# Mixture-of-experts loop of a decoder step: another place for the light experts, column groups in the second product, one merged product for the last two experts

## The reference

```
scores = sigmoid(x @ w_router);  idx = top 8 of the allowed groups;  gates = w_sel / sum(w_sel) * 2.5
for each expert e, with the tokens that chose it:
    hb = silu(xb @ w1_e[e]) * (xb @ w3_e[e])          # 1024 -> 256
    out[tokens] += (hb @ w2_e[e]) * gate              # 256 -> 1024
y = swiglu(x, w1_s, w3_s, w2_s) + out
x = layer_norm(ALPHA * x + y)
```

## Time and profile before

| | us |
|---|---|
| median of 3 runs | 1189.84 |
| lowest and highest | 1188.80, 1190.72 |
| the profiled execution | 1188.33 |
| its span | 1186.6 |
| expert loop, first c step to last y step, about | 535 to 1134 |
| loading back, sums and layer norm, about | 1127 to 1187 |

### The profile page before, as it was taken

How to read it: one execution, slowest core, us unless ns; L and a number is a source line. 1 busy time by engine, 2 the same in 40 slices (tenths; PEclk the granted TensorE clock), 3 DMA queues, 4 the chain that set the end, 5 groups by cost and what they waited for, 6 DMA issues and landing times.

```text
span 1186.6 us, 21423 instructions
## 1 busy us (share of the span) xinstructions
PE 1129.1 (95%) x8348; PEld 752.3 (63%) x8348; DVE 427.9 (36%) x1127; ACT 256.9 (22%) x533; POOL 254.0 (21%) x292
## 2 busy tenths in 40 slices
PE   7999996999999988989999999999999999999996
PEld 6888654877875767857765555555555565555521
DVE  0359998233039434661112222122222222221034
ACT  1101144013042124201122222222222222222210
POOL 3120050000000000032333333433323333333300
PEclk9999998999998999999999999999999999999999
DMA  9630304015045652185999999999999999999696
GB/s 331 250 142 1 152 21 177 1 75 227 1 143 176 250 214 108 73 286 197 365 408 392 396 383 394 402 399 388 383 386 402 393 384 384 381 401 387 260 369 279
DMA packets 67593, 319.16 MB, mean 269 GB/s; under 512 B 11591, under 2 KB 17951, under 8 KB 40909
## 3 DMA queue, kind: packets, MB, share of 16 engines
q1 hardware_dynamic: 51269, 278.60, 60.3%
q0 software_dynamic: 14848, 35.48, 7.9%
q10 hardware_dynamic: 1424, 4.35, 0.9%
HBM read 300.15 MB, written 29.36 MB: 278 GB/s over the span
## 4 chain that ended last, share of the span: by engine, by line
PE 74%; DVE 16%; DMA 4%; ACT 2%; SPq 2%; issue 1%; POOL 0%; DVEq 0%; POOLq 0%
PE psum L797 66%; PE psum L812 8%; DVE act_mem L1782 7%; DVE mk_mem L1944 2%; DMA arena<-y_rows 2%; DMA arena<-in_w_in_dram 1%; SPq L572 1%; DMA act_mem<-x_rows,more_x 1%; DVE act_mem L2000 0%; ACT act_mem L1565 0%; DVE act_mem L2151 0%; DVE act_mem L1879 0%; ACT act_mem L1574 0%; DVE act_mem L1796 0%; DVE act_mem L2163 0%
## 5 line engine op out<-in xcount | busy, mean ns | idle before, releaser
L797 PE MATMUL psum<-arena,act_mem 128*32 128x128 f32 (+6 forms) x4800 | 507.8, 361 | 0.9 <-ACT act_mem L1665 0.9
L797 PEld LDWEIGHTS psum<-arena,act_mem 128*32 128x32 f32 (+5 forms) x4800 | 259.7, 123 | 188.8 <-issue 107.9
L797 PE MATMUL psum<-act_mem,arena 128*128 128x260 f32 (+1 forms) x1728 | 355.1, 367 | 8.2 <-DMA arena<-in_w_in_dram 2.8
L797 PEld LDWEIGHTS psum<-act_mem,arena 128*128 128x128 f32 x1728 | 307.9, 194 | 52.8 <-DMA arena<-in_w_in_dram 3.0
L705 POOL DMA_INDIRECT y_rows<-act_mem,idx_y x39 | 45.9, 1177 | 239.3 <-DVE act_mem L2201 226.3
L812 PE MATMUL psum<-ident,act_mem 128*128 128x128 f32 (+6 forms) x484 | 80.0, 297 | 17.2 <-DVE act_mem L1883 6.8
L2201 DVE TENSOR_SCALAR act_mem<-psum,act_mem 96x512 f32<-96x512 f32 (+1 forms) x40 | 29.9, 747 | 159.7 <-PE psum L797 159.7
L1782 DVE SCALAR_TENSOR_TENSOR act_mem<-act_mem,wcb 128x511 f32<-128x511 f32 (+29 forms) x120 | 77.8, 729 | 0.0
L812 PEld LDWEIGHTS psum<-ident,act_mem 128*128 128x128 f32 (+6 forms) x484 | 58.5, 172 | 29.6 <-issue 13.7
L2198 DVE TENSOR_TENSOR act_mem<-act_mem,psum 128x192 f32<-128x192 f32 x35 | 12.4, 355 | 161.2 <-ACT act_mem L1636 161.2
L797 PEld LDWEIGHTS psum<-act_mem 128*96 128x96 bf16 (+7 forms) x419 | 31.3, 125 | 60.7 <-issue 59.7
(11 more groups left out here) (282 smaller groups left out, 789.6 us busy)
## 6 DMA issues: line engine op xcount, KB each, us to landing
arena<-in_w_e_dram SPq DMA_DIRECT2D x192, 1024.0 KB, 9.8
arena<-y_rows SPq DMA_DIRECT2D x8, 2048.0 KB, 24.2
arena<-in_w_in_dram SPq DMA_DIRECT2D x16, 512.0 KB, 18.0
arena<-in_cache_mem_k_dram SPq DMA_DIRECT2D x8, 1024.0 KB, 8.6
arena<-in_cache_mem_v_dram SPq DMA_DIRECT2D x8, 1024.0 KB, 12.1
arena<-in_w_v_dram SPq DMA_DIRECT2D x1, 4096.0 KB, 24.7
arena<-in_w_k_dram SPq DMA_DIRECT2D x1, 4096.0 KB, 14.0
arena<-in_w_out_dram SPq DMA_DIRECT2D x1, 4096.0 KB, 14.0
```

The costliest lines, as they stand in the source:

```text
L797: return pe.matmul(out, lhsT, rhs, start=first, stop=last)
```

## The change

The light places are now third, seventh and eighth of eight (`LIGHT = (2, 6, 7)`), so both of the last two experts are light, and the sixth place is heavy.

The down product of a heavy expert that isn't big is `down_most`: for 64 tokens two column groups of 64 side by side (4 products of 512 columns), for the other 32 tokens four column groups of 32 (8 products of 256 columns). Its result lies in pieces in PSUM, so `yh_most` copies it with three instructions on ACT and three on DVE, in place of one each. As tokens don't lie alone on partitions of that result in a way that one gate could be applied, the gate is now multiplied in DVE's `hd_most`, by two instructions with a per-partition factor in place of one; the factors are laid out by `spread_gates`, six small copies in `i_step`, before `idx_x` is written.

The last two experts' results go to `late_y`, expert 62 on partitions 0 to 63 and 63 on 64 to 127, and are added with 2 products of 128 rows a tile in place of 4. One of the three zero scatters goes.

```
-LIGHT = (2, 5, 7)
-HEAVY = (0, 1, 3, 4, 6)
+LIGHT = (2, 6, 7)
+HEAVY = (0, 1, 3, 4, 5)
...
+            def down_most(b, part):
+                _, wd = ew(part)
+                for k in range(2):
+                    for h in range(2):
+                        mm(psum[LCAP * h:LCAP * h + LCAP, 0, 0:512], hidT[:, b, MCAP * k:MCAP * k + LCAP],
+                           wd[:, k, 512 * h:512 * h + 512], k == 0, k == 1)
+                for k in range(2):
+                    for q in range(4):
+                        last = mm(psum[MORE * q:MORE * q + MORE, 0, 512:768], hidT[:, b, MCAP * k + LCAP:MCAP * k + MCAP],
+                                  wd[:, k, 256 * q:256 * q + 256], k == 0, k == 1)
+                return last
...
                 for h in range(2):
-                    mm(ps[0:w, 512 * h:512 * h + 512], slot_tok[0:MCAP, 0, t * P:t * P + w],
-                       ys[0:MCAP, 0, 512 * h:512 * h + 512], False, False)
-                for h in range(2):
-                    mm(ps[0:w, 512 * h:512 * h + 512], slot_tok[LCAP * h:LCAP * h + LCAP, 1, t * P:t * P + w],
-                       ys[LCAP * h:LCAP * h + LCAP, 1, 0:512], False, False)
+                    mm(ps[0:w, 512 * h:512 * h + 512], slot_tok[:, t * P:t * P + w],
+                       late_y[:, 512 * h:512 * h + 512], False, False)
...
+            def yh_most(out):                                     # DVE; ACT has the same for the other half
+                dve.tensor_copy(out[0:LCAP, 512:1024], psum[LCAP:2 * LCAP, 0, 0:512])
+                for q in range(2, 4):
+                    last = dve.tensor_copy(out[LCAP:MCAP, 256 * q:256 * q + 256], psum[MORE * q:MORE * q + MORE, 0, 512:768])
...
+            def spread_gates(n):
+                for h in range(2):
+                    dve.tensor_copy(gates[LCAP * h:LCAP * h + LCAP, n, 0:1], picked[0:LCAP, n, 1:2])
+                for q in range(4):
+                    dve.tensor_copy(gates[MORE * q:MORE * q + MORE, n, 1:2], picked[LCAP:MCAP, n, 1:2])
...
+            def hd_most(b, n):                                    # it was one tensor_tensor of 192 columns
+                dve.scalar_tensor_tensor(silu[:, b, 0:P], silu[:, b, 0:P], gates[:, n, 0:1],
+                                         psum[:, 2, 512 * b + 192:512 * b + 320], ALU.mult, ALU.mult)
+                return dve.scalar_tensor_tensor(silu[:, b, P:192], silu[:, b, P:192], gates[:, n, 1:2],
+                                                psum[:, 2, 512 * b + 320:512 * b + 384], ALU.mult, ALU.mult)
```

More of the change, by code:

```diff
@@ L243, in decoder_step @@
         swT = act_mem[:, A4 + 1296:A4 + 1296 + T]
+        gates = act_mem[:, A4 + 1860:A4 + 1860 + 2 * NB].rearrange("p (n c) -> p n c", c=2)
         idx_y = sb("idx_y", [P, NB], U32)
@@ L758, in _ @@
                     g_step(e + 3, (e + 3) % NB)
[L759 to L763, removed]
+                if SCATTERED <= e + 3 < E:
+                    scatter_halves((e + 3) % NB, zeros, s_zeroed)
             gp.wait_ge(s_over, 1)
@@ L1310, in y_step @@
                 else:
-                    down(n % 2, n % 4, CAP if is_big(e) else MCAP).then_inc(m_y, 1)
+                    (down if is_big(e) else down_most)(n % 2, n % 4).then_inc(m_y, 1)
             wait_out(pe, "x24")
@@ L1650, in yh, with yh_late @@
                 return act.activation(out[0:cap, 0:512], psum[0:cap, 0, 0:512], ACT.Copy, scale=picked[0:cap, n, 1:2])
+            def yh_late(b):
+                for h in range(2):
+                    last = act.activation(late_y[LCAP * b:LCAP * b + LCAP, 512 * h:512 * h + 512],
+                                          psum[LCAP * h:LCAP * h + LCAP, 0, 0:512], ACT.Copy)
+                return last
+            def yh_most(out):
+                act.activation(out[0:LCAP, 0:512], psum[0:LCAP, 0, 0:512], ACT.Copy)
+                for q in range(2):
+                    last = act.activation(out[LCAP:MCAP, 256 * q:256 * q + 256],
+                                          psum[MORE * q:MORE * q + MORE, 0, 512:768], ACT.Copy)
+                return last
             def sl_few(b):
@@ L1682, in y_step @@
                     act.wait_ge(m_sm[n % 2], 16 * halves_out(i, k - 2, 2))
-                if is_light(n):
+                if isinstance(e, int) and e >= SCATTERED:
+                    yh_late(e - SCATTERED).then_inc(m_ya, 1)
+                elif is_light(n):
                     yh_few(n % 2, n).then_inc(m_ya, 1)
+                elif is_big(e):
+                    yh(ys[:, n % 2, :], n).then_inc(m_ya, 1)
                 else:
-                    yh(ys[:, n % 2, :], n, CAP if is_big(e) else MCAP).then_inc(m_ya, 1)
+                    yh_most(ys[:, n % 2, :]).then_inc(m_ya, 1)
             def step(e, k, i, sc):
@@ L1709, in _ @@
             y_step(E - 1, NB - 1, LAST, 16 * ((E - 1) // 2))
-            for b, cap in enumerate((MCAP, P)):
+            for b in range(2):
                 wait_full(act, f"slots{b}")
-                act.activation(slot_tok[0:cap, b, :], bank(f"slots{b}")[0:cap, 0:T], ACT.Copy).then_inc(s_emA, 1)
+                act.activation(slot_tok[LCAP * b:LCAP * b + LCAP, :], bank(f"slots{b}")[LCAP * b:LCAP * b + LCAP, 0:T],
+                               ACT.Copy).then_inc(s_emA, 1)
             act.wait_ge(s_over, 1)
@@ L2178, in indices @@
                                       ALU.logical_shift_right)
+                if spread:
+                    spread_gates(n)
                 return dve.tensor_scalar(idx_x[0:cap, n:n + 1], idx_y[0:cap, n:n + 1], 3, None, ALU.logical_shift_right)
@@ L2227, in c_step @@
                     dve.wait_ge(m_y, e - 1)
-                (hd_few if is_light(n) else hd if is_big(e) else hd_most)(n % 2).then_inc(m_hd, 1)
+                if isinstance(e, int) and e >= SCATTERED:
+                    dve.wait_ge(m_idx, e + 1)
+                    hd_late(n % 2, n).then_inc(m_hd, 1)
+                elif is_light(n) or is_big(e):
+                    (hd_few if is_light(n) else hd)(n % 2).then_inc(m_hd, 1)
+                else:
+                    dve.wait_ge(m_idx, e + 1)
+                    hd_most(n % 2, n).then_inc(m_hd, 1)
             def y_step(e, k, i, sc):
```

28 lines of the change are left out of this document (17 added, 11 removed).

## The result

The changed kernel takes 1218.51 us (median of 4 runs, 1214.02 to 1222.03), the kernel before on the same chip 1190.2. The ratio is 1.024, with a 95% interval of 1.021 to 1.027: **slower by about 28 us**, where 1177.0 and a range up to 1187 had been predicted. The profiled execution has a span of 1212.2 us against 1186.6.

The account below looks back on a forecast made before the run. The prediction took TensorE's instructions to bound the loop. 20.9 us saved by the end of y(61), less 6.3 for late gathers and 1.7 at the end, gave 12.9: from 1189.84 to 1177.0 us, range 1167 to 1187.

Parts of the forecast that it names:

- The down product: TensorE's heavy down product: 3.43 us becomes 2.79, saving 0.64 each (0.58 to 0.70), 21.8 us over 34 products.
- SP's weight DMAs, ACT's queue and the order of the rest stay: Closing claim on indices and gates: these queues and the remaining order are unchanged; no cost was counted.
- Two signs of being wrong: Named as refuting the forecast: TensorE waiting at other gathers too; down products of 3 us or more.
- The gather that comes too late: GpSimd's gather for each eight's first expert leaves 5.5 us for landing; TensorE waits 7.5 us in all, +6.3 net.
- profit from the wait ahead of it: Claim that the gather of each eight's second expert gains from the first expert's wait, so no wait was counted.
- The DMA: Weight loading in the loop: dry 2.2 us an eight, so 14.6 us can go before the DMA is always busy.
- rival C: Gathers slow as the DMA loses its dry places; TensorE waits twice in each eight: 1197 us, chance 0.08.
- Rival B: The DMA is already full, so shorter products gain little in the loop: 1186.5 us, chance 0.12.
- Copying out: DVE's and ACT's copies of the down result grow about 0.7 us, hidden from TensorE; GpSimd's scatter starts later.
- The end: After the loop, the load back starts 5.8 us after y(61) in place of 4.2: +1.7 us (1.3 to 2.2).

Follow-up runs that it names:

- the best version: The kernel before with the column groups alone, TensorE's loop written out and GpSimd's gather ahead of its scatter, old order kept: 1174.64 us, ratio 0.988.

## Why the prediction was wrong

**The step that failed** isn't in the sum at all. "The down product" counts the time of 12 products in place of 4 and never what their number does to TensorE's program, a term that was put at nothing without a reason: 40 products, some 160 instructions, more in a block that is executed six times. The cost shown by the experiments is 26.4 us (the changed kernel against the one written out), 30.9 with the old order, 32 to 37 in the kernel before with its products cut. The rivals didn't hold it either: 1218.5 lies above even the waits for gathers twice an eight (1197), and for another reason. The paragraph with "SP's weight DMAs, ACT's queue and the order of the rest stay" is the place where the question belonged: which queues and memories does the change load? The earlier trace rows shows the number of instructions of before, and the page's line of queue 8 stood beside it.

That step is the larger part and not the whole. Written out, the changed kernel takes 1192.1 us, still outside the range that ended at 1187. The 15 us between it and 1177.0 are about the gathers (15.4 - 1.2 = 14.2 in place of 6.3), the down products (16.0 in place of 21.8) and one stretch at the lower clock (1.6). Two signs of being wrong that the prediction named came true: TensorE waits at other gathers too, and a heavy down product takes 2.87 us, above the 2.7 to 2.85 said, though not 3.

**The down product** was mis-sized. Measured are 2.87 - 1.87 = 1.00 us for the part of the 32 tokens, against 0.92 taken and 0.98 as the upper bound; the saving of the product itself is 0.56, below the lowest value given (0.58). A second term was missed: before, the down product behind b's transposes starts 1.00 us after them,

```profile
810.61 3.60 PE L797 MATMUL psum<-arena,act_mem 128*96 128x512 f32 x8
```

(809.61 to 810.61); the grouped one starts 812.20 to 813.28 = 1.08 after. A light one had shown this in the rows already (820.25 to 821.34 = 1.09). A saving of 0.56 - 0.09 = 0.47 for each of five gives 2.35 an eight: 75.1 would be 72.75, and 72.9 is measured. The 34 x 0.64 = 21.8 us were 34 x 0.47 = 16.0.

**The gather that comes too late** was right in mechanism and, for the experts that it names, in size: with the stops removed, TensorE waits for the rows of 16, 24 ... 56 for 7.0 us in all, where 7.5 had been worked out (2.2 for one of them and none for expert 48). What was missing are the others. Expert 8 costs 1.7. The fifth experts, for which nothing was counted, wait for 2.7. The second ones, which were to "profit from the wait ahead of it", wait for 4.0: their gather comes behind the scatter of the sixth place, which was light with one indirect DMA and is heavy with two. Together 15.4 us in place of 7.5 (added up over the timeline's rows of these transposes). The landings grew too, to a median of 8.3 us from 640 to 1100 us (the earlier trace rows has 7.7), so part of rival C was true. In the changed kernel as it is, TensorE waits at such transposes for 8.1 us, 2.1 of it with a gather named and 6.0 as "issue"; the stops hide the rest.

**The DMA** was right: in the best version the load back starts at 1111.48, 16 us earlier than before, without a wait for weights, and the DMA gave 405 GB/s over the loop (391 before). Rival B falls. **Copying out** was right: DVE's first copy is 0.69 us, the two others 0.43 each, 1.55 for 0.747; the scatter starts 2.72 after y (2.76 predicted). **The end**: 6.1 us from y(61) to the load back, 5.8 predicted; +1.9 for +1.7.

**The sum with the terms as measured**, up to the load back in the profiled executions: down products -16.0; y(61) heavy +1.0; TensorE's waits from 600 us on 26.8 - 1.2 = +25.6; the five stretches at the lower clock, four after the stops of about 4 us and one after the gather's 2.88, read from the products behind them (at 856.25, 863.93 - 856.25 = 7.68 in place of 822.40 - 816.29 = 6.11; and so on: 1.6, 2.7, 1.6, 1.7, 1.6), +9.2; the end +1.9; and +1.3 by which everything ahead of the loop happened to be later in this execution. That is 23.0 of 1152.78 - 1127.45 = 25.3 us. Some 2 us stay without a name.

## What to carry to other kernels

An edit that multiplies instructions has a cost that no row of the kernel before shows: count the instructions of the loop block, not of one product only, and read the instruction queue's line before and after. When a kernel on one engine stops at the same place in each turn with "issue" and nothing else, write the loop out; it costs little here (0.2%), as its instructions, read in a row, arrived in time. And when the bound engine gets faster, ask of each engine behind it in what order it does its two jobs: gather before scatter was worth 12.8 us in one order of the experts, 5.8 in another, and nothing in the kernel before.

## What the runs showed of the hardware

- **TensorE keeps a loop block of its program up to a size between 447 and 457 products here (about 1,660 to 1,700 instructions)**; a larger one is fetched again in each turn, nine packets or 0.147 MB with 477 products, and TensorE stands for some 4 us at each jump back (from 3.6 to 5.6 in the kernels above, and once 1.14, where the packet had come early). The 2048 instructions that the Trainium skill, Runtime: NRT & Kernel Launch, Instruction fetch mechanics, gives are above the 1,780 of the changed kernel; by that figure alone it would have fit, and the runs say that it doesn't. By the section's 16 KiB blocks 128 KiB are eight, and a turn here reads nine packets of that size, so the figure and the runs would agree if whole packets counted, with one read ahead; that is an estimate and no run tests it. The same section speaks of a window of two pages; the kernel before, with about 1,620 instructions in its block, read no packet between 690 and 1060 us, nearly five turns, so far more than two pages are kept.
- **Instructions without jumps were fetched with no stop here**: the best version reads 41 packets between 640 and 1080 us, and TensorE is busy in all of it.
- **A stop is paid twice.** After 4 us of nothing the granted clock is at 1.2 GHz for 3.4 us of work or, at 775.42, for about 6 (0.50 in both 775 to 778 and 778 to 781), which costs 1.6 to 2.7 us more. Single waits of 1.96, 2.23 and 2.88 us in the loop were followed by the same, one of 2.38 us (written out, at 917.44) was not, and none of the waits of 0.2 to 1.84 us was.

```profile
775.00:778.00 3.00, 2.58 (x12) 1.43 (x14) 0.00 (x0) 0.59 (x3) 0.91 (x1) 0.50 1.00 418
778.00:781.00 3.00, 3.00 (x17) 1.64 (x16) 0.00 (x0) 0.00 (x0) 0.00 (x0) 0.50 1.04 416
```
